# Key jobs of latent attention in another order, a value tile ahead of the last query turn, and ten unread products

## The chip, the cores and the metric

The kernel is one program on one core of a Trainium2 chip. The metric is the device time of one execution in microseconds (us). Before the change it is 1809.6 us, the median of 3 runs (1809.4 to 1811.5). The engines are called as in the profile: PE (TensorE, with its weight loads as PEld), DVE (VectorE), ACT (ScalarE), POOL (GpSimd) and SP (SyncE, which issues the weight loads from HBM).

## The reference

Two layers over 512 latent tokens and 256 context tokens of width 1024. Layer 0 mixes by a gated recurrence, layer 1 by multi-head latent attention; each is followed by a mixture of 16 experts. The change is in layer 1's attention, of which this is the core:

```python
def mla_qkv(h, w_in, q_norm, kv_norm, w_uq, w_ukv, cos, sin):
    z = h @ w_in                                  # 1024 -> 384 + 256 + 32
    cq, ckv, kr = z[..., :Q_LORA], z[..., Q_LORA:Q_LORA + KV_LORA], z[..., Q_LORA + KV_LORA:]
    q  = (rmsnorm(cq, q_norm) @ w_uq).reshape(B, L, 16, 96)
    kv = (rmsnorm(ckv, kv_norm) @ w_ukv).reshape(B, L, 16, 64 + 64)
    ...                                           # rotary part of q and kr, keys = [k_nope, kr]
def attend(q, k, v):
    s = jnp.einsum('bqhd,bkhd->bhqk', q, k) * ATTN_SCALE
    p = jax.nn.softmax(s, axis=-1)
    return jnp.einsum('bhqk,bkhd->bqhd', p, v)
k_all = jnp.concatenate([k_lat, k_ctx], axis=1)   # 512 + 256 = 768 keys
```

Only the 512 latent tokens ask (four query tiles of 128); all 768 tokens (six tiles) are keys and values.

## The kernel before

**Projection to latent space** (loop over `step`, from L1035). For each of six token tiles PE multiplies by `w_in` in split precision: for each of 8 depth blocks three products of 384 columns (queries, only for the four latent tiles) and three of 288 columns (keys). ACT takes the squares, DVE writes the normalised tile into `cqn` and counts `s_cqn`. In the same step PE turns the tile before: it waits for `s_cqn` (this tile is normalised) and for `s_cqT` (the tile before that one has been copied out of the same PSUM banks), and transposes `cqn` into `duo`; DVE copies it from there into `cqT` and `ckvT` (L2114, L2117). In step 4 the product is that of tile 4, and the tile turned is tile 3.

**Attention** runs over four groups of four heads (`for g in range(NG)`). A group begins with a stage that makes queries and keys, its order written out by hand on each engine:

- `q_project(g, t)` (L1121): query tile t, 3 products of 384 columns. DVE rotates it into `qtok` (`q_tile`, L2137 to L2144). `turn_queries(t)` (L610, turned<-qtok) waits for that. ACT copies the turned tile rounded (`q_hi`, L1538) and DVE writes the remainder (`q_lo`, `q_rest`, L2163).
- `k_project(j)` (L1099): key job j, a pair of heads by either the 512 latent columns or the 256 context columns. ACT copies it rounded (`k_hi`, L1544), DVE writes the remainder (`k_lo`, `k_rest`, L2156) and counts `s_kT`. All key jobs use one PSUM bank, so that job j+1 waits for the remainder of job j. `key_job` says which job is which.
- `v_project(t)` (L1112): one of six value tiles, copied out by DVE (`v_tile`, L2149). Tiles 0 and 1 have banks of their own.

Then come 16 units (head by query tile): `scores` (L1165, L1166), the softmax on DVE, ACT and POOL, `turn_probs`, and `values` (L1190). The last query products of a group are followed by the first of the next. The first scores of a group wait for the keys of the first pair of heads, the second pair is first read at unit 8.

DVE's order in the key stage is its own list: for t = 1, 2, 3 `q_tile(t)`, `q_rest(t-1)`, `k_rest(t-1)` (in group 0 also `turned_rest`, L2170, for the shared rotary part), then `v_tile(0)`, `v_tile(1)`, `q_rest(3)`, `k_rest(3)`. ACT's is `q_hi(t)`, `k_hi(t)` for t = 0 to 3.

The loads of weights for the experts of layer 1 are issued by SP from one list in order. They go into slots that attention's own weights hold until its last group is through.

`idle_products(bank, n)` issues n products of the identity by itself (128x128) into a PSUM bank that nobody reads.

Of the kernel before, what the change touches and what calls it, by code (L numbers as in the profile page):

```python
# [44 lines left out]
def build(nc, x, c, ctx, c_ctx, ada_w, ada_b, norm_mix, norm_ffn, norm_final, lru_w_in, lru_conv_w, lru_conv_b,  # L45
# [6 lines left out]
    TLT, TT = TL // P, T // P  # L52
# [60 lines left out]
    for n in range(KD):  # L113
        g, k0, k1 = SIDE[n]
# [78 lines left out]
    with ExitStack() as es:  # L193
# [3 lines left out]
        def sem(name):  # L197
            return es.enter_context(nc.semaphore(name))


        wide = es.enter_context(nc.psum_tensor("wide", [P, 4, BANK], F32))
# [65 lines left out]
        def flat(a, n, w):  # L267
# [86 lines left out]
        s_q, s_qtok, s_qtr, s_qT, s_kv, s_krt, s_krl, s_kT = [sem(n) for n in (  # L354
            "s_q", "s_qtok", "s_qtr", "s_qT", "s_kv", "s_krt", "s_krl", "s_kT")]
# [8 lines left out]
        def ring_at(name):  # L364
            return chunk_at(place[name][0])
# [56 lines left out]

        def key_job(j):

            pair, part = divmod(j, 2)
            cols_ = slice(0, TL) if part == 0 else slice(TL, T)
            return pair, cols_, cols_.stop - cols_.start

        def v_bank(t):

            return wide[:, 2 + t, 0:HG * VD] if t < 2 else duo[:, t % 2, 0:HG * VD]
# [5 lines left out]
        def mla_w(k):  # L437

            j = [n for n, (a, b) in enumerate(MLA_K) if a <= k < b][0]
            cols_ = slice((k - MLA_K[j][0]) * MZ, (k - MLA_K[j][0] + 1) * MZ)  # L440
            slot = place["mla_in", j][0]
            return ring[:, slot, cols_], mla_hi[:, k, :], ring_r[:, slot, cols_]
# [15 lines left out]
        def mla_lhs(t):  # L458

            tile = slice(t * P, (t + 1) * P)  # L460
            return hT2[:, :, tile], hT2_hi[:, t, :].rearrange("p (k n) -> p k n", k=KD), hT2_lo[:, :, tile]
# [19 lines left out]
        def unit(u):  # L481

            (pair, t), hh = divmod(u // 2, TLT), u % 2
            return 2 * pair + hh, t, pair, hh
# [113 lines left out]
        def _(pe):  # L598
# [6 lines left out]
            def turn(dst, src, plain=False):  # L605

                n = src.shape[0]
                if plain:
                    return mm(dst, src, ident[0:n, 0:n], start=True, stop=True)
                return nc.tensor.transpose(dst, src, ident[0:n, 0:n])  # L610

            def idle_products(bank, n):

                for _ in range(n):
                    mm(bank[:, 0:P], ident[:], ident[:], start=True, stop=True)
# [25 lines left out]
            def turn_tile(s, t, *owed):  # L641

                owed = list(owed)

                pe.wait_ge(s_xn, N0[s] + t + 1)
                for half, s_ev in ((0, s_hTa), (1, s_hTd)):
                    if t >= 1:

                        pe.wait_ge(s_ev, N0[s] + t)
                    for k in range(4):  # L650
                        f = (4 * half + k) * P
                        ins = turn(turned[:, half, k * P:(k + 1) * P], stages[s]["xn"][:, t, f:f + P])
                        if owed and k < 3:
                            ins.then_inc(owed.pop(), 1)
                    ins.then_inc(s_xtr, 1)
# [380 lines left out]
            for step in range(TT + 1):  # L1036
                if step < TT:
                    t = step
                    if t >= 2:

                        pe.wait_ge(s_cqn, t - 1)
                    else:

                        pe.wait_ge(s_ye[0], E + 1)
                        pe.wait_ge(s_modcol, 6)

                    pe.wait_ge(s_hlo, MLA_L0 + t + 1)
                    b = 2 * (t % 2)
                    _, lhs_hi, lhs_lo = mla_lhs(t)
                    for k in range(KD):  # L1050
                        if t == 0:

                            pe.wait_ge(s_wlo, MLA_W0 + k + 1)
                        _, w_hi, w_lo = mla_w(k)
                        for i, (lhs, w) in enumerate(((lhs_hi, w_hi), (lhs_lo, w_hi), (lhs_hi, w_lo))):
                            edge = dict(start=k == 0 and i == 0, stop=k == KD - 1 and i == 2)
                            if t < TLT:
                                mm(wide[:, b, 0:QL], lhs[:, k, :], w[:, 0:QL], **edge)
                            ins = mm(wide[:, b + 1, 0:MZ - QL], lhs[:, k, :], w[:, QL:MZ], **edge)
                        if t == TT - 1 and k in (2, 5):  # L1060
                            ins.then_inc(used[place[("mla_in", k // 3)][0]], 1)
                    ins.then_inc(s_mz, 1)

                    if step + 2 < TT:
                        turn_tile(2, step + 2)
                if step >= 1:
                    t = step - 1

                    pe.wait_ge(s_cqn, t + 1)
                    if t >= 1:  # L1070
                        pe.wait_ge(s_cqT, t)
                    for k in range(KQ if t < TLT else 0):
                        turn(duo[:, 0, k * P:(k + 1) * P], cqn[:, t % 2, k * P:(k + 1) * P])
                    for k in range(KKV):
                        ins = turn(duo[:, 1, k * P:(k + 1) * P], cqn[:, t % 2, QL + k * P:QL + (k + 1) * P])
                        if step == TT and k == 0:
                            ins.then_inc(used[place[("mla_in", 2)][0]], 1)
                    ins.then_inc(s_cqtr, 1)
# [10 lines left out]
            for g in range(NG):  # L1089

                def k_project(j):

                    pe.wait_ge(*((s_kT, g * 4 + (j + 1)) if j else (s_OT, g * 2 + 2)))
                    pair, cols_, n = key_job(j)
                    for k in range(KKV):
                        for h in range(2):
                            at = (g * HG + 2 * pair + h) * (NOPE + VD)
                            w = ring_at(("ukv", k))[:, at:at + NOPE]
                            ins = mm(duo[h * NOPE:(h + 1) * NOPE, 1, 0:n], w, ckvT[:, k, cols_], start=k == 0, stop=k == KKV - 1)  # L1099
                    ins.then_inc(s_kv, 1)  # L1100

                def v_project(t):

                    if t == 3:

                        pe.wait_ge(s_kT, g * 4 + 5)
                    if t >= 4:

                        pe.wait_ge(s_V, g * 6 + (t - 1))
                    for k in range(KKV):  # L1110
                        w = ring_at(("ukv", k))[:, g * BANK:(g + 1) * BANK].rearrange("p (h n) -> p h n", h=HG)[:, :, NOPE:NOPE + VD]
                        ins = mm(v_bank(t), ckvT[:, k, t * P:(t + 1) * P], w,  # L1112
                                 start=k == 0, stop=k == KKV - 1)
                    ins.then_inc(s_vp, 1)
# [11 lines left out]
                def turn_queries(t):  # L1126
                    pe.wait_ge(s_qtok, g * 4 + (t + 3))

                    if t >= 2:
                        pe.wait_ge(s_qT, g * 4 + t)  # L1130
                    for h in range(HG):
                        ins = turn(turned[:, t % 2, h * P:(h + 1) * P], qtok[:, t % 2, h, :])
                    ins.then_inc(s_qtr, 1)
# [4 lines left out]
                for t in range(1, TLT):  # L1138
                    q_project(g, t)
                    k_project(t - 1)  # L1140
                    turn_queries(t)
                v_project(0)
                v_project(1)
                k_project(TLT - 1)
                pe.wait_ge(s_krl, 3)
# [1 line left out]
                def scores(u):  # L1147
                    h, t, _, _ = unit(u)
                    if h == 0:

                        pe.wait_ge(s_qT, g * 4 + (t + 2))

                    if u == 0:
                        pe.wait_ge(s_kT, g * 4 + 3)
                    if u == 1:

                        pe.wait_ge(s_V, g * 6 + 2)
                    if u == 2 * TLT:
                        pe.wait_ge(s_krl, 4)
                    pe.wait_ge(s_exp, g * 16 + (u + 1))  # L1160
                    b = 2 * (u % 2)

                    for n, (q, k_) in enumerate(((q_hi, k_hi), (q_hi, k_lo), (q_lo, k_hi))):
                        q, edge = q[:, h, t * P:(t + 1) * P], dict(start=n == 0, stop=n == 2)
                        mm(wide[:, b, :], q, k_[:, h, 0:TL], **edge)  # L1165
                        ins = mm(wide[:, b + 1, 0:TC], q, k_[:, h, TL:T], **edge)  # L1166
                    ins.then_inc(s_S, 1)
# [1249 lines left out]
```

## Time and profile before

| | |
|---|---|
| median of the 3 runs | 1809.6 us |
| the profiled execution | 1811.66 us, span 1809.9 us |
| PE busy | 1666.5 us, 92% of the span |
| DVE, ACT, POOL busy | 39%, 29%, 10% |
| mean granted PE clock | 0.982 of full speed |
| projection to latent space | from 946 to 997 us |
| the four attention groups | from 998 to about 1250 us |

The span is the time between the first and the last recorded instruction; the execution's own time lies 1.8 us above it. Times in the views count from the start of the span. A figure in brackets behind a row of a timeline is the idle time of the engine just ahead of it, and what ended it. A granted clock of 1.00 is 2.4 GHz, and 0.50 is 1.2 GHz.

### The profile page before, as it was taken

To read this page: it belongs to the slowest core of one execution; us is meant where nothing else is said; L and a number is where in the kernel's file an instruction comes from. 1 tells how busy PE (TensorE), PEld (TensorE's weight loads), DVE (VectorE), ACT (ScalarE), POOL (GpSimd) and SP (SyncE) were. 2 spreads that over 40 slices of the span, in tenths; PEclk is the share of its full clock that TensorE was granted. 3 is DMA by queue.
4 is the path that set the end of the run, shared out by engine and by line. 5 is a ranking of instruction groups with operands and counts; after the bars stand their busy time and mean duration, and the time that the engine had idled before them with its cause. 6 is when DMAs were issued, how large, how long until landed. Compare 5 with 4: busy or idle time off the path is not lost.

```text
span 1809.9 us, 23194 instructions
## 1 busy us (share of the span) xinstructions
PE 1666.5 (92%) x9735; PEld 854.7 (47%) x9735; DVE 703.6 (39%) x1415; ACT 531.6 (29%) x902; POOL 182.4 (10%) x203
## 2 busy tenths in 40 slices
PE   4999989889999999999999899999959998888887
PEld 2666768543333333333358678778733332223222
DVE  4666765621221221221145665666441222122123
ACT  4777882300110110110144545546310000000002
POOL 1000010010010010010011225323000000000001
PEclk8999999999999999999999999999979999999999
DMA  9554361699999999999991100002589999999996
GB/s 365 195 210 166 118 237 77 267 347 404 403 404 385 403 402 385 403 402 385 413 333 60 49 1 1 1 1 104 190 350 421 421 421 421 422 421 420 421 421 257
DMA packets 89591, 520.76 MB, mean 288 GB/s; under 512 B 11347, under 2 KB 19648, under 8 KB 33936
## 3 DMA queue, kind: packets, MB, share of 16 engines
q1 hardware_dynamic: 80128, 487.74, 66.8%
q0 software_dynamic: 9360, 31.54, 5.6%
q8 instruction: 77, 1.26, 0.3%
q14 instruction: 26, 0.21, 0.0%
HBM read 502.37 MB, written 16.88 MB: 287 GB/s over the span
## 4 chain that ended last, share of the span: by engine, by line
PE 63%; SPq 20%; ACT 6%; DVE 5%; DMA 4%; issue 2%; ACTq 0%; DVEq 0%; POOLq 0%
SPq L539 20%; PE wide L927 15%; PE duo L982 7%; PE wide L938 6%; PE wide L694 6%; PE turned L610 5%; PE wide L783 4%; PE duo L994 3%; PE wide L1165 3%; PE duo L1190 2%; PE duo L1121 2%; DMA sb_ring<-moe_w_down 1%; DMA sb_ring<-ada_w 1%; PE wide L1166 1%; PE duo L1099 1%
## 5 line engine op out<-in xcount | busy, mean ns | idle before, releaser
L927 PE MATMUL wide<-sb_ring_x,sb_xT 128*64 128x512 f32 x1160 | 264.9, 598 | 18.3 <-DMA sb_ring_x<-moe_w_up 17.3
L927 PE MATMUL wide<-sb_ring,sb_xT 128*64 128x512 f32 x888 | 202.2, 597 | 13.0 <-DMA sb_ring<-moe_w_up 12.8
L927 PEld LDWEIGHTS wide<-sb_ring_x,sb_xT 128*64 128x64 f32 x1160 | 77.6, 136 | 187.2 <-issue 134.8
L982 PE MATMUL duo<-sb_ring_x,sb_hidT 128*64 128x512 f32 x536 | 124.3, 599 | 4.4 <-DMA sb_ring_x<-moe_w_down 4.4
L927 PEld LDWEIGHTS wide<-sb_ring,sb_xT 128*64 128x64 f32 x888 | 59.8, 136 | 143.8 <-issue 104.9
L1917 DVE TENSOR_TENSOR sb_hid<-wide,sb_sg 128x512 f32<-128x512 f32 x16 | 11.1, 691 | 300.0 <-ACT sb_sg_c L1435 300.0
L2382 POOL TENSOR_TENSOR sb_prob<-sb_prob,sb_asum 128x768 f32<-128x768 f32 x64 | 94.0, 1468 | 171.0 <-DVE sb_asum L2196 171.0
L982 PE MATMUL duo<-sb_ring,sb_hidT 128*64 128x512 f32 x424 | 99.9, 601 | 7.5 <-DMA sb_ring<-moe_w_down 7.3
L1433 ACT ACTIVATE sb_sg<-wide 128x512 f32<-128x512 f32 x16 | 9.6, 597 | 327.2 <-PE wide L938 327.2
L1917 DVE TENSOR_TENSOR sb_hid<-wide,sb_hid 128x512 f32<-128x512 f32 x16 | 11.1, 691 | 227.9 <-ACT sb_hid L1433 227.9
L1433 ACT ACTIVATE sb_hid<-wide 128x512 f32<-128x512 f32 x16 | 9.6, 597 | 252.3 <-PE wide L927 252.3
L982 PEld LDWEIGHTS duo<-sb_ring_x,sb_hidT 128*64 128x64 f32 x536 | 35.1, 136 | 79.0 <-issue 68.2
L694 PE MATMUL wide<-sb_hT_hi,sb_w_hi 128*128 128x512 f32 x240 | 65.5, 354 | 7.2 <-DVE sb_hT_lo L1699 7.2
L2357 POOL DMA_INDIRECT stream<-sb_ye,sb_idx_t x15 | 21.8, 1456 | 482.5 <-DVE sb_ye L1947 482.5
L2200 DVE TENSOR_REDUCE sb_asum<-wide 128x1 f32<-128x768 f32 x64 | 60.5, 946 | 15.2 <-PE wide L1166 15.1
L938 PE MATMUL wide<-sb_ring_x,sb_xT 128*32 128x512 f32 x568 | 65.6, 595 | 0.0
L1444 ACT ACTIVATE sb_hidT<-turned 128x512 f32<-128x512 f32 x31 | 18.4, 595 | 160.3 <-PE turned L610 160.3
L1566 ACT ACTIVATE sb_prob<-wide,sb_asum 128x768 f32<-128x768 f32 x64 | 57.7, 902 | 24.4 <-DVE sb_asum L2200 24.4
L694 PE MATMUL wide<-sb_hT_hi,sb_w_lo 128*128 128x512 f32 x240 | 62.8, 343 | 0.0
L694 PE MATMUL wide<-sb_hT_lo,sb_w_hi 128*128 128x512 f32 x240 | 62.2, 341 | 0.0
L982 PEld LDWEIGHTS duo<-sb_ring,sb_hidT 128*64 128x64 f32 x424 | 27.3, 136 | 67.4 <-issue 52.9
L1803 DVE TENSOR_TENSOR sb_x_b<-sb_x_b,wide 128x512 f32<-128x512 f32 x64 | 41.6, 683 | 45.0 <-PE wide L911 42.7
(447 smaller groups left out, 2811.2 us busy)
## 6 DMA issues: line engine op xcount, KB each, us to landing
sb_ring_x<-moe_w_up SPq DMA_DIRECT2D x145, 1024.0 KB, 28.8
sb_ring<-moe_w_up SPq DMA_DIRECT2D x111, 1024.0 KB, 27.8
sb_ring_x<-moe_w_down SPq DMA_DIRECT2D x69, 1024.0 KB, 27.8
sb_ring<-moe_w_down SPq DMA_DIRECT2D x59, 1024.0 KB, 27.4
sb_ring<-ada_w SPq DMA_DIRECT2D x40, 1024.0 KB, 7.4
sb_ring<-lru_w_in SPq DMA_DIRECT2D x8, 1024.0 KB, 9.1
sb_ring_x<-ada_w SPq DMA_DIRECT2D x8, 1024.0 KB, 17.1
sb_ring<-lru_w_out SPq DMA_DIRECT2D x4, 1024.0 KB, 6.4
```

Source lines behind the costliest of these rows:

```text
L539: sp.dma_start(dst, src).then_inc(landed[slot], 16)
L610: return nc.tensor.transpose(dst, src, ident[0:n, 0:n])
L694: ins = mm(banks[i], w[:, p % 2, k, :], seg(h[:, k, :], i), start=k == 0 and n == 0, stop=k == KD - 1 and n == 2)
L783: ins = mm(wide[:, b + n, :], lhs[:, k, :], w[:, n * BANK:(n + 1) * BANK], start=k == 0 and i == 0, stop=k == KD - 1 and i == 2)
L927: ins = mm(wide[n * CAPL:(n + 1) * CAPL, s, :], mine[:, k, :], w[:, at:at + BANK], start=k == 0, stop=k == KD - 1)
L938: ins = mm(wide[n * CAPC:(n + 1) * CAPC, 2, :], xT[:, k, CAPL:M], w[:, n * BANK:(n + 1) * BANK], start=k == 0, stop=k == KD - 1)
L982: ins = mm(lat[n * CAPL:(n + 1) * CAPL, :], hidnT[lay][:, 2 * (c % 2) + r, h * CAPL:(h + 1) * CAPL], w[:, r, n * BANK:(n + 1) * BANK], sta ...
L994: ins = mm(both[at:at + CAPC, :], hidT_c[:, 2 * (c % 2) + r, h * CAPC:(h + 1) * CAPC], w[:, r, n * BANK:(n + 1) * BANK], start=c == 0, sto ...
L1165: mm(wide[:, b, :], q, k_[:, h, 0:TL], **edge)
L1566: fn(prob[:, u % LAG, :], wide[:, b:b + 2, :].rearrange("p a n -> p (a n)")[:, 0:T], ACT.Exp, bias=asum[:, 0, u % 4:u % 4 + 1], accum_out= ...
L2200: v.tensor_reduce(asum[:, 0, u % 4:u % 4 + 1], wide[:, b:b + 2, :].rearrange("p a n -> p (a n)")[:, 0:T], AX_X, ALU.max, negate=True).then ...
L2382: g_.tensor_tensor(prob[:, u % LAG, :], prob[:, u % LAG, :], asum[:, 2, u % 4:u % 4 + 1].to_broadcast([P, T]), ALU.mult).then_inc(s_pn, 1)
```

## The change

Three edits. Key jobs are now numbered with both 512-column jobs first (job 0: pair 0 latent, 1: pair 1 latent, 2: pair 0 context, 3: pair 1 context), so that the first scores wait for three jobs and not for two. `v_project(0)` stands ahead of the last `turn_queries`, in each group. In step 4 of the projection to latent space ten unread products stand between PE's wait for `s_cqn` and its wait for `s_cqT`.

```diff
         def key_job(j):
 
-            pair, part = divmod(j, 2)
+            part, pair = divmod(j, 2)
             cols_ = slice(0, TL) if part == 0 else slice(TL, T)
             return pair, cols_, cols_.stop - cols_.start
...
                     pe.wait_ge(s_cqn, t + 1)
+                    if step == TT - 2:
+                        idle_products(wide[:, 2, :], 10)
                     if t >= 1:
                         pe.wait_ge(s_cqT, t)
...
                 for t in range(1, TLT):
                     q_project(g, t)
                     k_project(t - 1)
+                    if t == TLT - 1:
+                        v_project(0)
                     turn_queries(t)
-                v_project(0)
                 v_project(1)
                 k_project(TLT - 1)
...
                     if u == 0:
-                        pe.wait_ge(s_kT, g * 4 + 3)
+                        pe.wait_ge(s_kT, g * 4 + 4)
```

PE in the key stage of a group, from the second query product to the first scores. `cqT` is the queries' latent tile, `ckvT` that of keys and values, `qtok` the rotated query tile; line numbers of the kernel after are two or three higher. Before:

```order
L1121 MATMUL duo<-sb_ring,sb_cqT 128x384 x3
L1099 MATMUL duo<-sb_ckvT,sb_ring 64x256 x4
L610 MATMUL turned<-sb_ident,sb_qtok 128x128 x4
L1121 MATMUL duo<-sb_ring,sb_cqT 128x384 x3
L1099 MATMUL duo<-sb_ckvT,sb_ring 64x512 x4
L610 MATMUL turned<-sb_ident,sb_qtok 128x128 x4
L1112 MATMUL wide<-sb_ring,sb_ckvT 128x256 x4
L1099 MATMUL duo<-sb_ckvT,sb_ring 64x256 x4
L1165 MATMUL wide<-sb_k_hi,sb_q_hi 128x512
```

And the same stretch of PE after the change:

```order
L1123 MATMUL duo<-sb_ring,sb_cqT 128x384 x3
L1101 MATMUL duo<-sb_ckvT,sb_ring 64x512 x4
L610 MATMUL turned<-sb_ident,sb_qtok 128x128 x4
L1123 MATMUL duo<-sb_ring,sb_cqT 128x384 x3
L1101 MATMUL duo<-sb_ckvT,sb_ring 64x256 x4
L1114 MATMUL wide<-sb_ring,sb_ckvT 128x256 x2
L610 MATMUL turned<-sb_ident,sb_qtok 128x128 x4
L1114 MATMUL wide<-sb_ring,sb_ckvT 128x256 x2
L1101 MATMUL duo<-sb_ckvT,sb_ring 64x256 x4
L1168 MATMUL wide<-sb_k_hi,sb_q_hi 128x512
```

The key jobs of 256 and 512 columns have changed places around the third query turn, and one value tile (2 products) now stands ahead of the fourth. DVE over the same stretch, before:

```order
L2144 TENSOR_TENSOR sb_qtok<-sb_rtmp 128x2x2x8 x4
L2163 SCALAR_TENSOR_TENSOR sb_q_lo<-turned,sb_q_hi 128x4x128
L2156 TENSOR_TENSOR sb_k_lo<-duo,sb_k_hi 64x256 x2
L2137 COPY sb_qtok<-duo 128x2x2x64
L453 TENSOR_TENSOR sb_rtmp<-duo,sb_ropes 128x64 x4
L2144 TENSOR_TENSOR sb_qtok<-sb_rtmp 128x2x2x8 x4
L2163 SCALAR_TENSOR_TENSOR sb_q_lo<-turned,sb_q_hi 128x4x128
L2156 TENSOR_TENSOR sb_k_lo<-duo,sb_k_hi 64x512 x2
L2149 COPY sb_V<-wide 128x256 x2
```

And DVE after, over the same stretch:

```order
L2147 TENSOR_TENSOR sb_qtok<-sb_rtmp 128x2x2x8 x4
L2166 SCALAR_TENSOR_TENSOR sb_q_lo<-turned,sb_q_hi 128x4x128
L2159 TENSOR_TENSOR sb_k_lo<-duo,sb_k_hi 64x512 x2
L2140 COPY sb_qtok<-duo 128x2x2x64
L453 TENSOR_TENSOR sb_rtmp<-duo,sb_ropes 128x64 x4
L2147 TENSOR_TENSOR sb_qtok<-sb_rtmp 128x2x2x8 x4
L2166 SCALAR_TENSOR_TENSOR sb_q_lo<-turned,sb_q_hi 128x4x128
L2159 TENSOR_TENSOR sb_k_lo<-duo,sb_k_hi 64x256 x2
L2152 COPY sb_V<-wide 128x256 x2
```

DVE's steps keep their places; only the widths of the two remainders of keys are exchanged. PE in step 4 of the projection to latent space, after the change (before, the row of L615 is not there):

```order
L1059 MATMUL wide<-sb_mla_hi,sb_hT_hi 128x288
L1059 MATMUL wide<-sb_mla_hi,sb_hT_lo 128x288
L1059 MATMUL wide<-sb_ring_r,sb_hT_hi 128x288
L615 MATMUL wide<-sb_ident 128x128 x10
L610 MATMUL duo<-sb_ident,sb_cqn 128x128 x5
L1059 MATMUL wide<-sb_mla_hi,sb_hT_hi 128x288
```

The ten products come behind the last product of tile 4 and ahead of the turn of tile 3.

## Rows read from the trace of the kernel before

**Rows 1.** The page's chain that ended last, by engine (shares of the span).

```profile
PE 63%; SPq 20%; ACT 6%; DVE 5%; DMA 4%; issue 2%; ACTq 0%; DVEq 0%; POOLq 0%
```

**Rows 2.** What SP's DMA queue waited for, 1000 to 1300 us (total, times, longest).

```profile
SPq L539 <- PE turned L610: 256.9, 1, 256.9
```

**Rows 3.** What PE waited for, 1036 to 1250 us (total, times, longest).

```profile
PE turned L610 <- DVE sb_qtok L2144: 2.0, 3, 0.7
```

**Rows 4.** Timeline of PE, key stage of group 1 (start us, us, instruction).

```profile
1074.20 1.08 PE L1099 MATMUL duo<-sb_ckvT,sb_ring 128*64 128x256 f32 x8
1075.95 0.66 PE L610 MATMUL turned<-sb_ident,sb_qtok 128*128 128x128 f32 x4 [0.67 <-DVE sb_qtok L2144]
1076.45 2.10 PE L1121 MATMUL duo<-sb_ring,sb_cqT 128*128 128x384 f32 x6
1078.48 1.94 PE L1099 MATMUL duo<-sb_ckvT,sb_ring 128*64 128x512 f32 x8
1080.35 0.65 PE L610 MATMUL turned<-sb_ident,sb_qtok 128*128 128x128 f32 x4
1080.84 1.89 PE L1112 MATMUL wide<-sb_ring,sb_ckvT 128*128 128x256 f32 x8
1082.66 1.08 PE L1099 MATMUL duo<-sb_ckvT,sb_ring 128*64 128x256 f32 x8
1083.68 0.50 PE L1165 MATMUL wide<-sb_k_hi,sb_q_hi 128*128 128x512 f32 x1
```

**Rows 5.** Timelines of ACT and DVE, key stage of group 1.

```profile
1071.80 1.21 ACT L1544 ACTIVATE sb_k_hi<-duo 64x512 fp32r<-64x512 f32 x2 [3.22 <-PE duo L1099]
...
1072.42 1.39 DVE L2156 TENSOR_TENSOR sb_k_lo<-duo,sb_k_hi 64x512 fp32r<-64x512 f32 x2 [0.42 <-ACT sb_k_hi L1544]
1075.40 0.50 DVE L2144 TENSOR_TENSOR sb_qtok<-sb_rtmp 128x32 f32<-128x32 f32 x4
1076.42 0.85 DVE L2156 TENSOR_TENSOR sb_k_lo<-duo,sb_k_hi 64x256 fp32r<-64x256 f32 x2
1080.09 0.68 DVE L2163 SCALAR_TENSOR_TENSOR sb_q_lo<-turned,sb_q_hi 128x512 fp32r<-128x512 f32 x1
1082.51 0.76 DVE L2149 COPY sb_V<-wide 128x256 f32<-128x256 f32 x2
```

**Rows 6.** Timelines of PE and DVE, key stage of group 0.

```profile
1012.20 0.66 PE L610 MATMUL turned<-sb_ident,sb_qtok 128*128 128x128 f32 x4 [1.07 <-DVE sb_qtok L2144]
...
1009.58 0.95 DVE L2170 TENSOR_TENSOR sb_k_lo<-wide,sb_k_hi 64x768 fp32r<-64x768 f32 x1
```

**Rows 7.** Timeline of PE, end of the projection to latent space.

```profile
981.08 0.38 PE L1059 MATMUL wide<-sb_mla_hi,sb_hT_hi 128*128 128x288 f32 x1
...
984.23 0.29 PE L1059 MATMUL wide<-sb_ring_r,sb_hT_hi 128*128 128x288 f32 x1
987.93 1.30 PE L610 MATMUL duo<-sb_ident,sb_cqn 128*128 128x128 f32 x5 [3.40 <-DVE sb_ckvT L2117]
...
996.68 0.54 PE L610 MATMUL duo<-sb_ident,sb_cqn 128*128 128x128 f32 x2 [2.13 <-DVE sb_ckvT L2117]
997.02 1.51 PE L610 MATMUL wide<-sb_ident,sb_krope 128*128 128x128 f32 x6
998.56 3.00 PE L1121 MATMUL duo<-sb_ring,sb_cqT 128*128 128x384 f32 x6
1003.13 0.66 PE L610 MATMUL turned<-sb_ident,sb_qtok 128*128 128x128 f32 x4 [1.57 <-DVE sb_qtok L2144]
```

**Rows 8.** The chain of waits in order of time, tile 5's product.

```profile
989.22 5.12 PE wide L1059 x24
```

**Rows 9.** Busy time by stretch (us, busy PE, PEld, DVE, ACT, POOL, PE clock, DMA).

```profile
986.60:993.40 6.80, 5.47 (x24) 5.50 (x25) 3.25 (x13) 0.00 (x0) 0.00 (x0) 0.50 0.10 18
...
996.80:1000.20 3.40, 3.37 (x11) 2.26 (x11) 0.94 (x10) 1.62 (x2) 0.00 (x0) 0.50 0.93 336
```

**Rows 10.** Timeline of PE, unread products ahead of the projection to latent space.

```profile
927.97 10.88 PE L615 MATMUL duo<-sb_ident 128*128 128x128 f32 x96
```

## The prediction

> **What bounds the kernel now.** I read first the page's chain that ended last: PE holds 63% of it and SP's DMA queue 20% [rows 1]. The two follow one another. In attention PE is the chain, and in the last experts it is the stream of weights. So the next question is whether time saved in attention reaches the end, and the waits of SP's queue answer it: its next loads wait 256.9 us for one event on PE, the first instruction after attention's last group [rows 2]. The slots of the last experts' weights come free with that event, so the stream starts earlier by what attention ends earlier. I count savings ahead of that point in full.
>
> Then the waits of PE in groups 1 to 3: besides the work there are three waits of some 0.7 us, all for DVE's rotated query tile [rows 3]. The timeline of PE shows the place: the turn of query tile 2 starts at 1075.95 after 0.67 us idle, since the key job ahead of it is the short one [rows 4]. Group 0 has the same hole, 1.07 us [rows 6]. Last I read the end of the projection to latent space, where PE idles 3.40 us, then 2.13 us, and the granted clock stands at 0.50 (1.2 GHz) from 986.6 to 993.4 and from 996.8 to 1000.2 [rows 7, 9].
>
> **Key jobs and the value tile, groups 1 to 3.** The 512-column job takes PE 80.35 - 78.48 = 1.87 us from its start to the next instruction, the 256-column one 83.68 - 82.66 = 1.02; two value tiles take 82.66 - 80.84 = 1.82, one 0.91; a turn takes 0.50 and a query product 2.03 [rows 4]. With them I lay out group 1 anew, from 1074.20:
>
> The long job 1 ends at 1076.07. Query tile 2 was ready for its turn at 1075.95, so there is no wait. Turn to 1076.57, query product 3 to 1078.60, short job 2 to 1079.62, value tile 0 to 1080.53. Query tile 3 can be turned when? Tile 2 needed 1.75 us from the end of its product (1074.20) to its turn (1075.95), which gives 1080.35, if DVE begins in time. What is ahead of it on DVE is the remainder of job 1, now the long one. For job 0, ACT began at 1071.80 and DVE ended at 1072.42 + 1.39 = 1073.81, 2.01 us later [rows 5]. From 1076.12 that is 1078.13, ahead of 1078.60. So the turn starts at 1080.53 without a wait. Without the value tile there it would have waited 0.73 us: this edit is what keeps the hole from reappearing one turn later. Turn to 1081.03, value tile 1 to 1081.94, job 3 to 1082.96, then scores, where before they start at 1083.68: **0.72 us saved a group**, 2.2 us in three.
>
> The new condition is that job 2's remainder is done before job 3 and before the first scores. On DVE it follows query tile 3 (1080.30) and the query remainder (0.68), and takes 0.85 [rows 5]: 1081.83, while PE arrives at 1081.94. That is 0.1 us of slack, the thinnest point. Behind this wait PE holds job 3 and every score of the group, and if it is late by x, the group loses x. Before, the remainder of a long job stood there, and the value tiles ahead of job 3 hid it.
>
> **Group 0.** Here DVE has the shared rotary remainder (0.95 us) in front of query tile 2 [rows 6]. So the turn at 1012.20 does not move; the hole ahead of it shrinks from 1.07 to about 0.2. The gain comes behind it, where the short job stands for the long one: 0.85 us. Of this DVE takes back some, as its second rotary remainder follows the long job's remainder: 1012.20 + 0.7 (query remainder) + 1.39 + 0.95 = 1015.2, where query product 3 ends at 1014.7, so tile 3 is late by 0.2 beyond the cover of the value tile. I take **0.7**. Key stages together: 0.7 + 2.2 = **2.9 us**, with bounds of 0 (every hole moves to a later wait) and 1.07 + 3 x 0.73 = 3.3.
>
> **The ten unread products.** PE's last product ahead of the hole ends at 984.52, and the turn of tile 3 starts at 987.93 [rows 7]. 96 such products took 10.88 us, so ten take 1.13 us [rows 10]. `s_cqn` has been there by then (DVE normalised tile 3 while PE multiplied tile 4), so they run from about 984.4 to 985.6, inside the hole, and delay nothing; if the cover of 3.40 us were gone they would cost 1.13. By themselves they save nothing either. What they can change is the clock. Behind the 3.40 us of idleness the clock fell to 0.50, behind the 2.13 it fell again, behind the 1.57 at 1003.13 it did not [rows 7, 9]. The new hole is 3.40 - 1.13 = 2.3 us, nearer to 2.13 than to 1.57: the trace has a fall behind such a hole. But the fall need not come each time, nor last 6.8 us, since tile 5's product follows at once.
>
> The price of the two low stretches: PE was busy 5.47 and 3.37 us in them [rows 9], and at 2.4 GHz the same work would take half, so they cost 2.7 + 1.7 = 4.4 us. It is on the path: tile 5's product stands in the chain with 5.12 us [rows 8], where tile 4's took 984.52 - 981.08 = 3.44, and the first query product took 3.00 against 2.10 [rows 4, 7]. The gain of this edit lies between 4.4 us and a small loss, if the falls come at worse places.
>
> The Trainium skill ("TensorE: Matmul & The Clock Gate", Terms) puts the penalty of a low clock at its time by one minus the ratio, which would be (6.8 + 3.4) / 2 = 5.1 us here. The trace disagrees: for 1.36 us of that time PE had nothing to do [rows 9], so 4.4 stands; by the page's rule the most that can be won would be 0.7 more.
>
> **The sum.** By the profiled execution, 1811.66 us: minus 2.9, minus 4.4 if both low stretches go, is 1804.4. But that execution is 2.1 us above the median of the runs, 1809.6, and I know of nothing in it but the clock that could differ between runs. If the median run lacks 2.1 us of low clock, it has 2.3 of it left, and 1809.6 - 2.9 - 2.3 gives 1804.4 too. As falls behind holes of 2.1 to 2.3 us remain likely, I take half of the 2.3: 1809.6 - 2.9 - 1.2 = **1805.5 us**.
>
> The same page says (Part 1, the clock gate) that how many products run cold differs between runs of one kernel. No row here can show it, for there is one trace. It would fit the 2.1 us, and no term above uses it.
>
> **The rivals.** 0.2% is 3.6 us, about what a measurement of this kernel can tell from no change.
>
> - *The holes go, the clock is as before* (26%): 1809.6 - 2.9 = 1806.7. For it: the fall behind 2.13 us. Against: the first, longest hole loses a third.
> - *The clock stays high throughout* (18%): 1804.4 or somewhat under it. For it: 1.57 us did no harm. Against: the second hole, 2.13 us, is not touched by any edit.
> - *The holes move* (10%): DVE bounds the key stage, and PE waits at the turn of tile 3 or ahead of job 3 by most of what it saved. Only half of 2.9 and little of the clock is left: 1809.6 - 1.4 = 1808.2. For it: the slack of 0.1 us. Against: DVE has the same total of work, and idle time.
> - *Slower* (4%): the remainder of job 2 is what the first scores wait for, and DVE reaches it late in each group. If the copies of the value tiles (0.76), the query remainder (0.68) and the remainder itself (0.85) all lay behind PE's arrival, a group would lose 2.3 us; four of them 9.2, less the 2.9 won: 1815.9. It costs more than it saves from 0.7 us a group on. Against it: on DVE the value copies stand behind that remainder.
>
> **How the numbers follow.** The forecast's own case has 42%. The range reaches from 1803.5 (a quiet clock) to 1808.6 (holes moved), and leaves out the slower case and the ends of the others. Faster by more than 0.2% means below 1806.0: two thirds of the forecast's case, all of the quiet clock, a third of the case with the old clock, together 0.55. Within 0.2%: 0.41. Slower: 0.04.
>
> **What would show it right or wrong.** In the timeline of PE after: no wait for the rotated query tile in groups 1 to 3, about 0.2 us of it left in group 0 at the third turn, and the first scores of a group 0.7 us nearer to its first turn. A wait at the fourth turn, or ahead of key job 3, would show that the hole has moved. At 984 us, ten products in a hole that still ends with DVE's copy. In the stretches from there to the first query turn, fewer microseconds at 0.50; the same time at 0.50 leaves the gain to the key stages alone. The prediction is wrong in its frame if the first instruction after attention comes 4 us earlier and the end does not.

## The result, and the profile after

The changed kernel takes 1805.15 us, the median of 11 runs (1804.40 to 1806.74), where the kernel before takes 1809.6 (11 runs, 1807.58 to 1811.72). The ratio is 0.9978, with a 95% interval of 0.9970 to 0.9986, 2.5 to 5.4 us. Run again, beside 21 runs of the kernel before, the ratio was 0.9976 (0.9967 to 0.9985), and its trace had the clock fall at the same single place, for 3.4 us behind the 2.13 us hole. The forecast was 1805.5 us. The profiled execution took 1806.74 us, its span 1805.0.

The page's chain has hardly moved, and SP still waits for the end of attention before it loads on. In the chain by engine and in the waits of SP's queue (compare [rows 1, 2]):

```profile
PE 63%; SPq 20%; ACT 6%; DMA 4%; DVE 4%; issue 2%; ACTq 0%; DVEq 0%; POOLq 0%
```

```profile
SPq L539 <- PE turned L610: 254.8, 1, 254.8
```

What PE waited for in groups 1 to 3 (1036 to 1250 us; total, times, longest) no longer names the rotated query tile of [rows 3]:

```profile
PE turned L610 <- ACT sb_PT L1561: 1.1, 2, 0.6
```

The timeline of PE in the key stage of group 1, which answers to [rows 4] (start us, us, instruction):

```profile
1071.22 1.94 PE L1101 MATMUL duo<-sb_ckvT,sb_ring 128*64 128x512 f32 x8
1073.09 0.66 PE L610 MATMUL turned<-sb_ident,sb_qtok 128*128 128x128 f32 x4
1073.58 2.10 PE L1123 MATMUL duo<-sb_ring,sb_cqT 128*128 128x384 f32 x6
1075.61 1.08 PE L1101 MATMUL duo<-sb_ckvT,sb_ring 128*64 128x256 f32 x8
1076.63 1.13 PE L1114 MATMUL wide<-sb_ring,sb_ckvT 128*128 128x256 f32 x4
1077.59 0.60 PE L610 MATMUL turned<-sb_ident,sb_qtok 128*128 128x128 f32 x4
1078.03 1.03 PE L1114 MATMUL wide<-sb_ring,sb_ckvT 128*128 128x256 f32 x4
1078.99 1.08 PE L1101 MATMUL duo<-sb_ckvT,sb_ring 128*64 128x256 f32 x8
```

There is no bracket, thus no idle time of note. From the start of key job 1 to the start of key job 3 it takes 7.77 us, and before 1082.66 - 1074.20 = 8.46: 0.69 less. DVE's side, which answers to [rows 5]:

```profile
1073.83 1.39 DVE L2159 TENSOR_TENSOR sb_k_lo<-duo,sb_k_hi 64x512 fp32r<-64x512 f32 x2 [0.31 <-ACT sb_k_hi L1547]
1075.72 0.43 DVE L2140 COPY sb_qtok<-duo 128x256 f32<-128x256 f32 x1 [0.50 <-PE duo L1123]
1077.83 0.85 DVE L2159 TENSOR_TENSOR sb_k_lo<-duo,sb_k_hi 64x256 fp32r<-64x256 f32 x2
```

The long remainder is done at 1075.22, half a microsecond before DVE needs itself for query tile 3, and the remainder of job 2 at 1078.68, 0.3 us before PE comes for it at 1078.99.

The timeline of PE at the end of the projection to latent space, which answers to [rows 7]:

```profile
983.98 2.39 PE L615 MATMUL wide<-sb_ident 128*128 128x128 f32 x20
987.46 0.77 PE L610 MATMUL duo<-sb_ident,sb_cqn 128*128 128x128 f32 x5 [1.08 <-DVE sb_ckvT L2120]
...
993.76 0.41 PE L610 MATMUL duo<-sb_ident,sb_cqn 128*128 128x128 f32 x2 [2.13 <-DVE sb_ckvT L2120]
994.11 0.85 PE L610 MATMUL wide<-sb_ident,sb_krope 128*128 128x128 f32 x6
995.51 3.86 PE L1123 MATMUL duo<-sb_ring,sb_cqT 128*128 128x384 f32 x6 [0.56 <-DVE sb_marks L1601]
1000.95 0.66 PE L610 MATMUL turned<-sb_ident,sb_qtok 128*128 128x128 f32 x4 [1.57 <-DVE sb_qtok L2147]
```

Ten unread products are twenty recorded matmuls and last 2.3 us. The hole behind them is 1.08 us, not 2.3. Tile 5's product stands in the chain of waits with 3.21 us where [rows 8] has 5.12:

```profile
988.22 3.21 PE wide L1059 x24
```

And the busy time by stretch (length, busy PE, PEld, DVE, ACT, POOL, PE clock, DMA) shows the clock at 1.00 up to the second hole, and one stretch of 3.4 us at half of it:

```profile
983.90:995.80 11.90, 8.13 (x62) 7.36 (x62) 6.83 (x29) 3.18 (x8) 0.12 (x1) 1.00 0.43 149
995.80:999.20 3.40, 3.40 (x6) 1.35 (x4) 0.00 (x0) 2.08 (x2) 0.00 (x0) 0.51 0.93 353
```

I divide each trace by three marks on PE: the turn of tile 3, the first query turn of group 0, and the first instruction after attention (L610, 32x32).

| profiled execution | start to turn of tile 3 | to first query turn | to end of attention | to end | span |
|---|---|---|---|---|---|
| before | 987.9 | 15.20 | 250.93 | 555.9 | 1809.9 |
| after | 987.5 | 13.49 | 248.07 | 556.0 | 1805.0 |
| difference | -0.5 | -1.71 | -2.86 | +0.1 | -4.9 |

The two middle columns hold what the change touches, 4.57 us. All of it reaches the end: what follows attention takes 555.9 and 556.0 us here. In single traces this last stretch lies anywhere from 553.5 to 557.4 us, but its mean is 555.6 us over the ten traces with the new key stage and 555.6 over the four without, so an earlier end of attention isn't lost behind it.

### The profile page after: what moved, and what is told of

The parts are those of the page before. It is cut to its first block, busy times and chain, and to the rows that moved or that the text cites. A ratio compares the mean times of both kernels' runs of the same rounds, so it can differ in the third digit from the quotient of the medians.

```text
span 1805.0 us, 23233 instructions
## 1 busy us (share of the span) xinstructions
PE 1667.1 (92%) x9755; PEld 854.7 (47%) x9755; DVE 703.5 (39%) x1415; ACT 531.9 (29%) x902; POOL 183.0 (10%) x203
## 4 chain that ended last, share of the span: by engine, by line
PE 63%; SPq 20%; ACT 6%; DMA 4%; DVE 4%; issue 2%; ACTq 0%; DVEq 0%; POOLq 0%
SPq L539 20%; PE wide L927 15%; PE duo L982 7%; PE wide L938 6%; PE wide L694 6%; PE turned L610 5%; PE wide L783 4%; PE duo L994 3%; PE wide L1168 3%; PE duo L1193 2%; PE duo L1123 2%; DMA sb_ring<-moe_w_down 1%; DMA sb_ring<-ada_w 1%; PE wide L1169 1%; PE duo L1101 1%
```

## The experiments

Theory: two separate gains. The key stages give 2.9 us and need both the swap and the value tile. The unread products give 1.7 us and more, as they take a fall of the clock away. Rivals: the key stages are the whole gain and the clock moved by chance; the key order alone would do; any work in a hole would do. The results of all kernels stand in one table: the ratio to the kernel before on the same chip, with its interval, and the three middle numbers of their traces.

| kernel | median us (runs) | ratio, 95% interval | tile 3 to first query turn | to end of attention |
|---|---|---|---|---|
| changed, again | 1804.14 (11) | 0.9976 (0.9967 to 0.9985) | 13.50 | 248.09 |
| e1 keys and value tile only | 1805.79 (11) | 0.9980 (0.9971 to 0.9989) | 15.34 | 248.03 |
| the same, second time | 1805.98 (12) | 0.9991 (0.9981 to 1.0000) | 14.23 | 248.05 |
| e2 products only | 1806.33 (11) | 0.9988 (0.9979 to 0.9997) | 13.40 | 250.92 |
| e3 key order only | 1808.69 (11) | 1.0001 (0.9992 to 1.0010) | 15.28 | 250.80 |
| e4 five products | 1803.49 (6) | 0.9971 (0.9959 to 0.9983) | 14.16 | 248.05 |
| the same, second time | 1804.56 (7) | 0.9973 (0.9962 to 0.9984) | 13.36 | 248.08 |
| e5 second hole too | 1803.34 (5) | 0.9967 (0.9954 to 0.9980) | 11.80 | 248.11 |
| e6 mark first | 1804.22 (8) | 0.9974 (0.9964 to 0.9984) | 13.07 | 248.06 |
| e7 e5 and e6 | 1803.59 (7) | 0.9969 (0.9958 to 0.9980) | 11.45 | 248.06 |
| e8 value tile only | 1808.39 (12) | 0.9995 (0.9986 to 1.0004) | 15.26 | 250.95 |
| e9 third hole too | 1803.25 (5) | 0.9967 (0.9953 to 0.9980) | 11.45 | 248.06 |

The kernel before had medians of 1809.6, 1808.74, 1809.74 and 1807.89 us in the four groups of runs, so ratios are to be compared and not medians. The attention column repeats to 0.15 us: 248.03 to 248.11 in ten traces with the swap and the value tile, 250.80 to 250.95 in the four others. A trace tells 0.7 us a group apart where times of whole runs, which spread over 2 to 8 us, cannot.

**The key stages alone (e1).**

```diff
                     pe.wait_ge(s_cqn, t + 1)
-                    if step == TT - 2:
-                        idle_products(wide[:, 2, :], 10)
```

> Key jobs in the new order and the value tile ahead of the last query turn, without the unread products. Theory (two separate gains): all holes of the key stages go (0.8 us in group 0, 0.7 in each other group), the 3.40 us hole at 984 us stays, and a low-clock stretch behind it; 1809.6 - 2.9 = 1806.7 us, runs spread over 3 us or more. Rival (the key stages are the whole gain, and the clock moved by chance): as fast as the changed kernel, 1805.2 us, with the same narrow spread. Rival (the key stages give nothing that reaches the end): 1809.6.

Measured: 250.93 went to 248.03, the full 2.9 us, and the stretch ahead of it stayed at 15.34 with its 3.40 us hole and two low stretches. The times agree: 0.9980. The first rival, that this is the whole gain, falls by the trace and not by times: the interval overlaps that of the changed kernel. I ran it again.

> The key stages alone once more, beside the others of this chip. Theory: 2.9 us below the kernel before, and two low stretches in this trace or none, as the executions go. Rival: the difference of the first time was the chip's, and it is under 2 us here.

The ratio was 0.9991, which is 1.6 us with an interval from 0 to 3.4. By times this is what the rival asked for, under 2 us, and the 2.9 us lie inside the interval all the same. The trace decides: the attention stretch was 248.05 again. In this trace the 3.40 us hole was there, and the low stretch behind it lasted 3.4 us, not 6.8, so that 14.23 us stand where 15.34 did, with the same kernel. It is one source of the spread of runs, and at 1.1 us a small one beside the 5 to 7 us over which the runs of e1 spread.

**The products alone (e2).**

```diff
                     pe.wait_ge(s_cqn, t + 1)
+                    if step == TT - 2:
+                        idle_products(wide[:, 2, :], 10)
                     if t >= 1:
```

> The ten unread products alone, key stages as in the kernel before. Theory: the products are recorded as 20 matmuls and last 2.3 us, not the 1.13 that I predicted; the hole shrinks from 3.4 to 1.1 us and the clock does not fall behind it; the fall behind the 2.13 us hole can stay. 1809.6 - 1.6 = 1808.0 us, and a narrower spread than before. Rival (key stages are the whole gain): 1809.6 us, and the spread of before (4 us).

Measured: 13.40 us for 15.20, attention unchanged at 250.92, ratio 0.9988. The two gains are separate, and they add up: 1.80 + 2.90 = 4.70 in the traces of the parts, 4.57 in that of the whole. My spread was wrong: runs went over 4.3 us, and the repeated changed kernel over 5.5 us. The narrow 2.3 us of its first 11 runs was luck.

**The key order without the value tile (e3).**

```diff
-                    if t == TLT - 1:
-                        v_project(0)
                     turn_queries(t)
+                v_project(0)
                 v_project(1)
```

The unread products are left out here too.

> Key jobs in the new order alone: no unread products, and the value tile stays behind the last query turn. Theory: the hole reappears one turn later, 0.7 us ahead of the turn of query tile 3 in groups 1 to 3 and some 1.1 us in group 0, and nothing is saved in the key stages: 1809.6 us. Rival (the order of the key jobs alone does it, the value tile is not needed): no wait at that turn, 1806.7 us.

The hole moves by one turn, as the waits of PE in groups 1 to 3 say (total, times, longest):

```profile
PE turned L610 <- DVE sb_qtok L2144: 2.0, 3, 0.7
```

It is the same row as [rows 3], and only the timeline tells that it is at another turn, that of query tile 3, here in group 0 and then in group 1:

```profile
1012.11 1.08 PE L1099 MATMUL duo<-sb_ckvT,sb_ring 128*64 128x256 f32 x8
1013.85 0.66 PE L610 MATMUL turned<-sb_ident,sb_qtok 128*128 128x128 f32 x4 [0.66 <-DVE sb_qtok L2144]
...
1077.59 0.66 PE L610 MATMUL turned<-sb_ident,sb_qtok 128*128 128x128 f32 x4 [0.66 <-DVE sb_qtok L2144]
```

Attention took 250.80 us, the ratio is 1.0001. In group 0 I had expected 1.1 us and found 0.66.

**The value tile without the key order (e8).** The kernel before, with the value tile where its hole was:

```diff
                     k_project(t - 1)
+                    if t == 2:
+                        v_project(0)
                     turn_queries(t)
-                v_project(0)
                 v_project(1)
```

> The kernel before with value tile 0 ahead of the turn of query tile 2, where its hole is; key jobs in their old order, no unread products. Theory (the swap is needed): the hole at that turn goes in groups 1 to 3, but the long job 2 now has only one value tile between it and job 3, and its remainder ends 2.1 us behind it, so that PE waits some 0.7 us ahead of key job 3: no gain, 1809.6 us. Rival (any work in the hole will do): no wait there, 1806.7 us, as the key order with the value tile.

Again the hole moves, this time to the key job, in the waits of PE in groups 1 to 3 and in the timeline of group 1:

```profile
PE duo L1099 <- DVE sb_k_lo L2157: 2.0, 3, 0.7
```

```profile
1075.70 1.94 PE L1099 MATMUL duo<-sb_ckvT,sb_ring 128*64 128x512 f32 x8
1077.57 0.66 PE L610 MATMUL turned<-sb_ident,sb_qtok 128*128 128x128 f32 x4
1078.06 1.03 PE L1112 MATMUL wide<-sb_ring,sb_ckvT 128*128 128x256 f32 x4
1079.76 1.08 PE L1099 MATMUL duo<-sb_ckvT,sb_ring 128*64 128x256 f32 x8 [0.66 <-DVE sb_k_lo L2157]
```

The long job's remainder is not ready when only one value tile covers it. 250.95 us, ratio 0.9995: nothing is won. The new key order alone moves the hole to the next query turn, a value tile in the old hole moves it to the key job, and only the new order with a value tile ahead of the fourth turn closes it. The other literal half of the edit, the old key order with the value tile ahead of the fourth turn, wasn't run.

**Five products for ten (e4).** `idle_products(wide[:, 2, :], 5)`, in the changed kernel.

> The changed kernel with five unread products for ten, the 1.13 us of fill on which my prediction was made. The hole left is 3.4 - 1.1 = 2.2 to 2.3 us. Theory: the clock falls behind it in some executions, as behind the 2.13 us hole; 1805.5 to 1806 us, a spread wider than that of the changed kernel (2.3 us). Rival (any cut of the 3.40 us hole is enough): as the changed kernel, 1805.2 us.

> Five unread products once more, for a second trace and more runs. Theory: a 2.2 us hole, behind which the clock falls in some executions and not in others; median within 1 us of the changed kernel's. Rival (five do as well as ten): no fall in this trace, and a median at or under that of ten products.

Five products are what I had in mind when I forecast: the hole left is 2.20 us. In both traces the clock fell behind it. The first one by stretch, the turn of tile 3 being at 984.45:

```profile
985.20:988.60 3.40, 3.40 (x17) 3.40 (x16) 1.38 (x5) 0.00 (x0) 0.00 (x0) 0.51 0.11 8
988.60:992.10 3.50, 1.54 (x12) 1.31 (x10) 1.27 (x5) 0.77 (x3) 0.00 (x0) 0.99 0.91 363
992.10:995.50 3.40, 3.17 (x10) 2.36 (x11) 0.97 (x11) 1.25 (x1) 0.00 (x0) 0.50 0.95 359
```

In the second trace the fall came at the turn itself, and then none behind the 2.13 us hole: 13.36 us in all, as good as with ten. By times five and ten cannot be told apart (0.9971 and 0.9973 against 0.9978 and 0.9976), so the rivals' claim on the median is not refuted. By traces five leave a fall behind this hole in two of two, where ten leave none in seven. What remains after ten, one low stretch, is also all that the second trace with five has.

**The second hole too (e5).**

```diff
                 if step >= 1:
                     t = step - 1
 
+                    if step == TT:
+                        idle_products(wide[:, 2, :], 8)
                     pe.wait_ge(s_cqn, t + 1)
```

> The changed kernel with eight more unread products (16 recorded matmuls, 1.8 us) in the 2.13 us hole, ahead of the wait for tile 5's normalised rows. Theory: that hole shrinks to 0.3 us and the low stretch behind it goes; the first query product takes 2.1 us and not 3.9, and 1.0 to 1.7 us are won over the changed kernel, 1803.8 us. Rival (the fall comes of more than this hole, or the 1.57 us hole behind it takes over): a low stretch from some 999 us on, no gain.

The timeline of PE shows the second hole filled as well, 0.34 us of it left, and the first query product at full speed:

```profile
990.44 1.95 PE L615 MATMUL wide<-sb_ident 128*128 128x128 f32 x16
992.73 0.41 PE L610 MATMUL duo<-sb_ident,sb_cqn 128*128 128x128 f32 x2 [0.34 <-DVE sb_ckvT L2122]
993.08 0.85 PE L610 MATMUL wide<-sb_ident,sb_krope 128*128 128x128 f32 x6
994.48 2.17 PE L1125 MATMUL duo<-sb_ring,sb_cqT 128*128 128x384 f32 x6 [0.56 <-DVE sb_marks L1603]
```

The whole stretch stands at 1.00, and takes 11.80 us for 13.49: 1.69 us less, one low stretch's worth.

```profile
983.00:998.20 15.20, 11.67 (x82) 9.83 (x81) 8.27 (x38) 5.14 (x9) 0.00 (x0) 1.00 0.54 198
```

**The mark first (e6), and both (e7).**

```diff
             dve.wait_ge(s_cqT, TT)
+            mark(s_OT, 2)
             dve.wait_ge(s_rope, 16)
             v.memset(qtok[:] ...
-            for s_, n in (..., (s_PTd, 1), (s_OT, 2)):
+            for s_, n in (..., (s_PTd, 1)):
```

> The changed kernel with DVE's mark that frees the first query product's bank put first of its marks and ahead of the cleared query tile. Theory: the new 0.56 us wait of the first query product is for that mark, which was hidden while PE was slower; the wait goes to 0.1 us or less, and 0.4 us are won where the clock is high, half hidden elsewhere: 1804.8 us, not to be told by times. Rival (the wait is for the copy of tile 5's rows, and the mark only comes with it): the wait stays at 0.5 us.

> Both: the second hole filled, and the mark first. Theory: 1.5 to 2.1 us below the changed kernel, 1803.3 us, with a spread of runs of 2 us or less. Rival (low stretches elsewhere in the program decide the spread): same median as the second hole alone, and the spread of the changed kernel.

In e6 the wait of the first query product fell from 0.56 to 0.21 us, and the stretch from 13.49 to 13.07. So the wait was for the mark, for the greater part. My 0.1 us was too low. In e7 it is 11.45 us, 2.04 less than the changed kernel and 3.75 less than the kernel before. Runs of e7 spread over 2.7 us, not the 2 or less I had written.

**The third hole (e9).** e7 with `idle_products(wide[:, 2, :], 6)` between the first query product and its turn in group 0.

> As e7_both, with six more unread products (1.4 us) in the third hole, 1.57 us ahead of the first query turn. Theory: the clock does not fall there anyway, nothing is won, 1803.6 us. Rival (that hole is the one left that makes the clock fall in some executions): 1 us faster and a narrower spread.

The hole went from 1.57 to 0.23 us, and the stretch stayed at 11.45. Nothing is won, as the clock does not fall there. Its five runs spread over 4.9 us, so what is left of the spread lies elsewhere.

## Why the prediction was right, point by point

- **What bounds the kernel** held. Attention ended 2.86 us sooner from its first turn on, and from its end to the end of the span it is 555.9 us before and 556.0 after.
- **Groups 1 to 3** held: 0.72 us a group was worked out, 0.69 measured, no wait at any query turn. The lay-out of group 1 agrees by row: PE's wait for the remainder of job 2, which I called the thinnest point with 0.1 us of slack, had 0.3.
- **Group 0** held: a rest of 0.22 us before the third turn where I had 0.2. The stage from its first turn to its first scores went from 16.79 to 15.99 us, 0.8 for the 0.7 taken. DVE's second rotary remainder did not make tile 3 late.
- **The ten products** were mis-sized, and this is the step that failed. I took the x96 of [rows 10] for 96 products. The code ahead of that row issues 48, each recorded as two matmuls of this number format, so that ten last 2.3 us and not 1.13, and the hole left is 1.08 us and not 2.3. The direction, that they delay nothing and work by the clock alone, was right. With the wrong size I left a fall behind this hole likely. It did not come in any of the seven traces with ten products. With five, the size that I had in mind, it came in two of two.
- **The price of the clock** was right in kind and too high by a tenth for the first low part. From the turn of tile 3 to the second hole PE took 6.62 us before and 4.18 after, 2.44 less where 2.7 stood. I had halved the busy time, but a product of 288 columns doesn't take half at the high clock: PE starts one every 0.24 us at 1.2 GHz and every 0.13 us at 2.4, as these rows of the trace before show, first at the low clock, then at the high one:

```profile
990.22 0.44 PE L1059 MATMUL wide<-sb_ring_r,sb_hT_hi 128*128 128x288 f32 x1
990.46 0.44 PE L1059 MATMUL wide<-sb_mla_hi,sb_hT_hi 128*128 128x288 f32 x1
...
993.51 0.29 PE L1059 MATMUL wide<-sb_mla_hi,sb_hT_lo 128*128 128x288 f32 x1
993.64 0.30 PE L1059 MATMUL wide<-sb_ring_r,sb_hT_hi 128*128 128x288 f32 x1
```

- **What waits behind a faster PE** I had not looked at. Of the 2.44 us the stretch keeps 1.71: 0.56 go to a new wait of the first query product for DVE's mark, and some 0.2 to a second low stretch that costs more. Before, the clock had fallen 1.7 us ahead of this product, so that its end ran at the high clock, 3.00 us. After, the product starts 0.3 us ahead of the fall (995.84), and nearly all of it runs at 1.2 GHz, 3.86 us. The mark stood there all the time. DVE's marks, before and after:

```profile
998.21 0.11 DVE L1598 MEMSET sb_marks<- 128x1 f32 x7
...
995.16 0.11 DVE L1601 MEMSET sb_marks<- 128x1 f32 x7
```

  In both traces the query product starts 0.24 us after the last of them (at 998.56 and 995.51). Before, the six turns ahead of it took 1.51 us at the low clock and lasted until then; after, they take 0.85 and PE stands idle.
- **The rule on the penalty.** e5 against the changed kernel prices a single low stretch in which PE is busy throughout: 3.4 us of it cost 1.69. The rule of the Trainium skill ("TensorE: Matmul & The Clock Gate", Terms), time at the low clock by one minus the ratio, gives an estimate of 1.7. Here the trace agrees. For the first low stretch, 6.8 us, the same rule gives an estimate of 3.4, and 2.44 were won: PE idled in 1.3 us of it, and its products were slower by a factor of less than two.
- **The sum** hit 1805.15 with 1805.5, and partly by luck. Two errors cancel: the fill was twice what I thought, and the clock's gain was cut by the new wait and the dearer second stretch. That I took half of 2.3 us for the clock was a choice and no derivation. In traces it was 1.7. Its premise, that the median run lacks 2.1 us of low clock here, is not borne out: of the five traces with the 3.40 us hole (this stretch is the same code in all) four have the whole low time (15.20 to 15.34 us) and one 1.1 us less. Executions also differ by some 4 us ahead of this stretch and as much behind attention, which I had left out. And the medians themselves move: in the second comparison they lie 5.6 us apart, not 4.45, with nearly the same ratio.
- **The rivals.** "The holes go, the clock is as before" is what e1 built: 0.9980 and 0.9991. "The clock stays high throughout" is e5 and e7: the second hole, which I held against it, is indeed what keeps it from happening. "The holes move" happened in e3 and e8, and in neither part of the changed kernel. "Slower" did not come, as the remainder of job 2 is done 0.3 us ahead of key job 3.

## What to carry to other kernels

A hole in an order written by hand is closed only if the next two waits are checked as well: here the new order by itself moved 0.7 us to the next query turn, and a value tile by itself moved them to the key job. Unread products in a wait pay for the clock that follows, so size them by the recorded duration of one call, and look behind the faster stretch for what its slowness hid. Where runs of one kernel spread by 2 to 8 us and an edit is worth 1 to 3, three marks in a trace tell what medians don't.

By this stretch of the traces the best of the kernels here is e7, the change with the second hole filled and the mark first (e9 equals it): 2.04 us less than the changed kernel, and a time of 0.9969 (0.9958 to 0.9980) of the kernel before. Its interval overlaps that of the changed kernel, so by times it is not shown to be faster than it.

## What the runs showed of the hardware

Over all traces of this stretch, falls of the granted clock to 1.2 GHz by the length of PE's idle time ahead of them:

| idle time of PE | traces with such a hole | clock fell at or behind it |
|---|---|---|
| 1.08 us | 7 | 0 |
| 1.57 us | 13 | 0 |
| 2.13 us | 11 | 10 |
| 2.20 us | 2 | 2 |
| 3.40 us | 5 | 5 |

Behind the 3.40 us hole the low stretch lasted 6.8 us in four traces and 3.4 in the fifth, of the same code. I had expected the falls behind holes of some 2 us to be a matter of chance; they came nearly every time.

The table is no rule on the length of a hole. Each length but those of the first hole belongs to one place of the program, and elsewhere the count is another: at some 262 us, in layer 0, all 14 traces have a hole of 2.70 us, longer than the 2.13, and the clock fell behind it in 11 of them and not in 3 (a hole of some 1.7 us, seven us ahead of it, had no fall in any). The products that end that hole, in the kernel before, where the clock fell at 266.4, and in the second trace of the changed kernel, where it didn't:

```profile
265.30 4.56 PE L754 MATMUL wide<-sb_wo_a,sb_ring_r 128*128 128x512 f32 x12 [2.70 <-ACT sb_wo_a L1356]
...
264.29 3.04 PE L754 MATMUL wide<-sb_wo_a,sb_ring_r 128*128 128x512 f32 x12 [2.70 <-ACT sb_wo_a L1359]
```

So such a fall is one part of the spread of runs. What makes the rest of the spread is open: from the start to the turn of tile 3 the traces lie between 984.5 and 988.7 us, and from the end of attention to the end between 553.5 and 557.4, in stretches that no kernel here changed.
